# Ten matmuls without use between two groups of v rows in a PEER decoder step

## The reference

```python
def one_block(xt):                                  # xt: tokens x 1024
    q = (xt @ w_query).reshape(blk, 8, 256)
    s1 = einsum('nhd,hkd->nhk', q[..., :128], k1)   # 128 keys on each side
    s2 = einsum('nhd,hkd->nhk', q[..., 128:], k2)
    ...                                             # the best 16 of the 16 x 16 sums, per head
    experts = e1 * 128 + e2                         # 8 heads x 16 picks = 128 experts per token
    gate = softmax(top_sc)
    act = gelu(einsum('nd,nhkd->nhk', xt, u_tab[experts]))
    z = gate * act
    return einsum('nhk,nhkd->nd', z, v_tab[experts])
```

## Time and profile before

| | |
|---|---|
| median of 3 runs | 1845.31 us |
| the 3 runs | 1840.83, 1845.31, 1845.37 us |
| span of the profiled execution | 1822.2 us |
| what a run's time has beyond that span | 18.6 to 23.2 us |
| PE busy | 1105.9 us, 61% of the span |
| POOL busy | 1088.7 us, 60% |
| DVE busy | 1060.3 us, 58% |
| DMA | 643.92 MB, mean 353 GB/s |

### The profile page before, as it was taken

The page is one execution under the profiler, slowest core; times in us unless marked ns, Lnnn a source line. Parts: engine busy times, 40 slices in busy tenths (PEclk is TensorE's granted clock), DMA queues, the critical chain, the costliest instruction groups (busy, mean ns, idle before and its releaser), DMA issues.

```text
span 1822.2 us, 16621 instructions
## 1 busy us (share of the span) xinstructions
PE 1105.9 (61%) x5557; PEld 544.7 (30%) x5557; DVE 1060.3 (58%) x2708; ACT 273.3 (15%) x660; POOL 1088.7 (60%) x1194
## 2 busy tenths in 40 slices
PE   9766999987787789963433367543433344343345
PEld 8764444445665575540000011100000000000011
DVE  5454776737575484876677848764647444444420
ACT  3332144303210242210000000000000000000000
POOL 5523355655536555667666666666666766666664
PEclk9887998999878899996565578755565566665657
DMA  7777698999998999999999899999999999999997
GB/s 244 270 256 286 246 345 327 381 363 354 389 336 321 373 370 386 407 414 385 366 364 363 343 360 385 355 372 375 370 370 388 382 365 367 384 365 371 372 371 295
DMA packets 178652, 643.92 MB, mean 353 GB/s; under 512 B 21728, under 2 KB 21736, under 8 KB 178440
## 3 DMA queue, kind: packets, MB, share of 16 engines
q0 software_dynamic: 156672, 570.49, 80.8%
q1 hardware_dynamic: 21320, 70.28, 10.7%
q10 hardware_dynamic: 576, 2.10, 0.3%
HBM read 637.24 MB, written 5.16 MB: 353 GB/s over the span
## 4 chain that ended last, share of the span: by engine, by line
PE 31%; DVE 22%; POOL 17%; another core or an unknown queue 14%; issue 13%; ACT 2%; DMA 1%; ACTq 0%; DVEq 0%; POOLq 0%
PE pp L754 14%; POOL ring L714 8%; DVE ring L1229 6%; PE y L1046 4%; PE pp L764 4%; POOL w_ring L714 3%; PE pp L835 2%; POOL C_sample L714 2%; POOL act_T L714 2%; DVE w_ring L1229 2%; DVE act_T L1229 1%; DVE C_sample L1229 1%; POOL keys_T L714 1%; DVE lists L1558 1%
## 5 line engine op out<-in xcount | busy, mean ns | idle before, releaser
L714 POOL DMA_INDIRECT ring<-in_u_experts,expert_idx x316 | 302.0, 956 | 296.9 <-issue 79.3
L714 POOL DMA_INDIRECT ring<-in_v_experts,expert_idx_by_token x342 | 328.2, 960 | 224.3 <-issue 90.0
L1229 DVE SCALAR_TENSOR_TENSOR ring<-ring,x_normed 128x1024 f32<-128x1024 f32 x316 | 372.2, 1214 | 112.5 <-DMA ring<-in_u_experts,expert_idx 76.1
L1046 PE MATMUL a<-ring,z_columns 128*32 128x512 f32 x660 | 213.8, 957 | 184.3 <-DMA ring<-in_v_experts,expert_idx_by_token 110.7
L754 PE MATMUL pp<-act_T,w_ring 128*128 128x128 f32 (+2 forms) x1280 | 288.6, 387 | 13.2 <-ACT act_T L1889 5.7
L1046 PE MATMUL y<-ring,z_columns 128*32 128x512 f32 x792 | 226.6, 763 | 85.2 <-DMA ring<-in_v_experts,expert_idx_by_token 51.2
L754 PEld LDWEIGHTS pp<-act_T,w_ring 128*128 128x128 f32 x1280 | 198.4, 202 | 104.3 <-issue 96.7
L1046 PE MATMUL a<-w_ring,z_columns 128*32 128x512 f32 x124 | 79.3, 956 | 74.3 <-issue 35.9
L764 PE MATMUL pp<-w_ring,act_T 128*128 128x128 f32 (+1 forms) x832 | 108.2, 289 | 20.4 <-issue 9.4
L1046 PEld LDWEIGHTS a<-ring,z_columns 128*32 128x32 f32 x660 | 37.5, 146 | 275.7 <-issue 274.6
L764 PEld LDWEIGHTS pp<-w_ring,act_T 128*128 128x128 f32 (+1 forms) x832 | 100.7, 184 | 34.0 <-issue 31.4
(11 more groups left out here) (354 smaller groups left out, 1820.7 us busy)
## 6 DMA issues: line engine op xcount, KB each, us to landing
w_ring<-in_w_all SPq DMA_DIRECT2D x104, 512.0 KB
ring<-in_v_experts,expert_idx_by_token POOLq DMA_INDIRECT x342
ring<-in_u_experts,expert_idx POOLq DMA_INDIRECT x316
ring<-in_w_all SPq DMA_DIRECT2D x8, 512.0 KB, 9.1
x_res<-in_x_prompt SPq DMA_DIRECT2D x4, 512.0 KB, 7.2
C_sample<-in_state_C SPq DMA_DIRECT2D x4, 512.0 KB
out_C_s<-C_sample ACTq DMA_DIRECT2D x4, 512.0 KB
out_y_p<-x_res SPq DMA_DIRECT2D x16, 128.0 KB
```

The source lines that it names most:

```text
L714: pool.indirect_dma_start(out=slot[s], out_offset=None, in_=a["u_experts"] if kind == "u" else a["v_experts"], in_offset=bass.IndirectOffs ...
L1046: ins = pe.matmul(total[low:low + 32, half * 512:(half + 1) * 512], zcols[:, part % 2, lo:lo + 32], rhs, start=False, stop=True, skip_grou ...
L1229: dve.scalar_tensor_tensor(out=slot[s], in0=slot[s], scalar=1.0, in1=xn_now[:, :], op0=ALU.mult, op1=ALU.mult, accum_out=dots[:, part % 4, ...
```

## The change

`experts` gets a second argument. In the last call, the one for all that is left, and for each prompt tile from its 33rd pick on, PE issues after each group of four v rows ten matmuls of the identity with the constant tensor `blank` (288 columns, named `perm_fold` in the profile). They write the first 288 columns of the PSUM sum that is not in use (`Y` while the tile's own sum is in `A`, and the other way round), which nobody reads. Before them stands a wait until the earlier tile's result was taken from that sum. `v_done` is raised before the ten matmuls.

```diff
+BETWEEN = 10
...
-            def experts(upto):
+            def experts(upto, apart=False):
...
                     ins.then_inc(v_done, 4)
+                    if apart and t and n >= FIRST[t] + PART:
+                        other = Y if t in SECOND_SUM else A
+                        pe.wait_ge(y_ready, EO[t])
+                        for _ in range(BETWEEN):
+                            pe.matmul(other[:, 0:128 + NS + 128], ident[:, :], blank[:, :], start=True, stop=True)
                 done[0] = max(done[0], upto)
...
-            experts(TOTAL // 4)
+            experts(TOTAL // 4, True)
```

## The result

The changed kernel takes 1880.88 us (median of 4 runs, 1875.74 to 1891.45), beside 1845.34 us for the kernel before in the same session: a ratio of 1.0196, with a 95% interval of 1.016 to 1.0233. It is 35.5 us slower where 14.2 us were forecast. The direction and the range held, the size did not.

The account below looks back on a forecast made before the run. Late in the kernel, gathers bound it: eight per 9.9 us round, PE waiting. Rounds cost 0, the end 11.7 + 2.5 = +14.2 us on 1845.31, giving 1859.5 us; own range 1852 to 1869, 8 in 10 1845 to 1896.

Parts of the forecast that it names:

- The wait on `y_ready`: Before the added matmuls: the earlier tile's result is taken 14 us or more ahead of need, so cost 0.
- The fill behind the very last group: At the very end: its 5.0 us lie beside ACT, DVE and the store (7 us), so cost 0.
- the term of 11.7 us: Last eleven groups: 6.9 us of PE work against 4.96 us of gathers, so PE ends +11.7 us later.
- 18.6 to 23.2 us beyond the span: Whole run: what a run's time has beyond the profiled span was taken to stay unchanged.
- the crawl term of the end: Last eleven groups: a stretch of slow PE records adds +2.5 us, a third of 7.4; bounds 0 and 7.4 us.
- a cover: Rounds before the end: PE's 7.62 us wait for landings, of which the added matmuls fill 5.0 to 6 us.
- In the rounds of eight gathers: Before the last eleven groups: PE needs 6.9 to 8.1 us of each 9.9 us round, so cost 0.
- 122 us to give back: All 71 groups: by the skill's clock rule, each gets 1.72 us faster; the forecast counted none of it.
- crawls grow with PE's instructions: Rival, chance 0.23: more PE records make slow stretches earlier and POOL's 16 long waits longer, +24 us, 1883 us in all.

Follow-up runs that it names:

- the hold at the end: Changed kernel, but from pick 488 of v on POOL waits for the landing of the gather issued four before: 1873.86 us, ratio 1.0143.
- the two runs that leave the rounds alone: Changed kernel with the ten matmuls only from pick 500 on, 1878.83 us; changed kernel with forty no-operations in place of the ten matmuls, 1845.24 us.

## Why the prediction was off

**What held.** The direction (slower, 0.80). The clock rose, if not to the 0.8 to 1.0 that I named: 0.57 to 0.77 from 1250 to 1510 us, 0.84 from 1610 us on, 1.00 at the end, with v groups of 1.92 us there and, where the clock was full, in the rounds too (1782.41). The wait on `y_ready` costs nothing (1.0012 with the 71 waits alone). The fills' own time at the end: starts 6.9 us apart from 1834.98 on, and with the crawls taken away (the hold at the end) 72.6 us from the start of group 500 to PE's end (1790.9 to 1863.5), where the term of 11.7 us had 71.1. The fill behind the very last group (1871.35) lies beside ACT and the store. The time forecast, 1859.5 us, also took 18.6 to 23.2 us beyond the span; it goes by the median of before and does not hang on them.

**The step that failed is the crawl term of the end.** I took a third of one old crawl, +2.5 us, bounds 0 and 7.4, "because POOL is held back only after its free slots are used up". It measured 20.7 us (32.4 - 11.7); 22.1 us in two crawls where the fill stands at the end alone; and with four in flight there, and so without crawls, 19.7 us of it are gone. In the changed kernel 15.1 of the 20.7 us are a PE that is late when the end begins (26.4 us from issue to start instead of 11.3), from a crawl that begins in the fill behind group 496, one group ahead of the eleven, where the forecast had a cover and a cost of 0. The other 5.7 us are lost within the eleven (76.8 us instead of 71.1).

Three things were wrong in the term. The first is a reading: the bound of 7.4 us came from the shorter of the two crawls in the old end. The longer one stood in the same timeline of PE before, and the earlier trace rows leave it out:

```profile
1790.23 1.02 PE L1046 MATMUL y<-w_ring,z_columns 128*32 128x512 f32 x2 [1.63 <-DMA ring<-in_v_experts,expert_idx_by_token]
...
1801.88 1.01 PE L1046 MATMUL y<-w_ring,z_columns 128*32 128x512 f32 x1 [1.79 <-issue]
...
1806.32 1.03 PE L1046 MATMUL y<-C_sample,z_columns 128*32 128x512 f32 x1
```

This group took 16.1 us instead of 3.64, so 12.4 us were lost. The old kernel could hide that, since four groups then followed in 9 us; with the fill nothing hides it. The two old crawls in full are 19.9 us, near the 20.7. The second is the length: I treated it as PE's own. But `v_done` comes late in a crawl, POOL goes on issuing as long as it has free slots, and PE comes out of it when POOL has stopped and the unfinished gathers have become few (3.2 at the start of a crawl and 1.4 at its last late record in the kernel after, medians). That a crawl lasts for as long as the queue is long is argued from this, not shown by itself; crawls of up to 19 us stand in the trace of after. The third: I let a crawl meet eleven groups with 32 instructions. With the fill they have 72. A crawl still comes each 140 or so records, but from 1300 to 1400 us the trace has 595 of PE's records after and 306 before, so that is some 23 us now instead of 45, and at the end PE has no idle time with which to catch up.

**In the rounds of eight gathers** I took 0; it is some 7 us (2.6 to 11.6). PE does have its cover there, and the bare fills cost nothing that shows: with four in flight and no crawls the ratio is 1.0775 with the fill and 1.0794 without. What is left is POOL's waits behind pick 168: 45 of 3.3 us after and 41 of 3.6 us without fill at the end, 147 us in sum for each, against 26 of 5.2 to 5.3 us and 134 to 138 us in sum in the two runs that leave the rounds alone. More of them, each shorter. (The 16 waits with 80.0 us of the earlier trace rows were only a part of this: the waits for `ring` that the profile puts down to no engine and no DMA.) The page "TensorE: Matmul & The Clock Gate" of the Trainium skill, section "HAM oscillation — how this bites in real kernels", had 122 us to give back here; the groups did get faster, from 3.64 to 1.92 us, and nothing of it came back.

**The rival "crawls grow with PE's instructions"** had the mechanism (0.23), and its 1883 us are near the 1880.88, but for another reason: it put 24 us on sixteen waits in the rounds and left the end at 14. My argument against it was 740 to 780 us, where PE got through 379 records in 40 us with no crawl at a full DMA share. That argument missed that POOL pauses there each 12 us or so:

```profile
748.13 0.94 POOL L714 DMA_INDIRECT ring<-in_u_experts,expert_idx  x1 [3.58 <-DVE ring L1229]
...
763.92 0.93 POOL L714 DMA_INDIRECT ring<-in_u_experts,expert_idx  x1 [2.78 <-PE a L1046]
...
775.81 0.94 POOL L714 DMA_INDIRECT ring<-in_u_experts,expert_idx  x1 [2.20 <-PE a L1046]
```

From the end of one pause to the next PE has some 100 to 140 records, and about 1.5 gathers are unfinished after the first two. The emptied queue showed that a pause in which the queue runs dry begins the count anew. That one which only shortens it does so too fits these rows, and was not tested by itself.

**What stays open.** Why PE crawls. The runs show what it takes: some 130 of PE's records since the last pause or crawl, and a stream of gathers of which more than three are unfinished for much of the time. Which of the two, the length of the queue or the load on the DMA engines (a share of 0.91 with four in flight, 0.95 with six), is not told apart. They also show that PE's semaphore updates are late as well, from before the first late record on. Late instructions could be a cause, but the queue for instructions has 11 more packets (45 to 56) for 2840 more records, one for 258, and crawls come each 140. Only 4 of the 19 crawls before and 4 of the 35 after have one of its packets between 1 us ahead of their start and their end, and with four in flight and the fill the same 56 packets come and no crawl. The page "NOTIFIC — the notification-queue block", section "7.1 Overflow: three behaviours, one of which stalls the engine", of the Trainium skill says that the path that records events can hold an engine back when it fills. It would fit a count of records that must be written out beside the gathers; all runs here were recorded, so none can tell, and the crawl may be a matter of the recording.

## What to carry to other kernels

Before giving an engine idle work, find the place where its cover ends: here 60 of the 71 fills cost 7 us, and the last eleven cost 34. Cost idle work in instructions and not only in time: ten matmuls of 32 columns, which fit in the gaps, cost 1.2%, and that is not their own time (in recorded executions, which all of these were). Before a bound is taken from one slow place in a trace, look for the longest one of its kind. And a faster engine behind a saturated DMA stream was worth nothing here; the clock rose, and no microsecond came of it.

## What the runs showed of the hardware

- PE has a state in which matmul records stand 0.7, 1.4, 2.1 or 2.8 us apart. It was seen in v groups (1406.10 to 1410.30 us before), in fills of 288 columns (1786.46 to 1793.46 us with the fill at the end alone), and in the run with 32 columns (42 crawls). From one to the next there are 127 to 140 of PE's records and 10 to 42 us (medians of the ten kernels that crawl and don't empty the queue).
- With four gathers in flight it did not come at all, with or without the fill. With the queue emptied each 24 gathers it came once without the fill (some 96 records between two) and 24 times with it (some 216).
- With it PE's semaphore updates come late: that of `v_done` for group 496 at 1796.79 us, for work that ended at 1784.3; with four in flight never over 1.2 us after the last matmul.
- Four gathers of 512 KB in flight give 323 GB/s, six give 370 GB/s, nearly the 373 GB/s without a limit.
- To let the gather queue run dry and start it again costs POOL 6.4 us a time.
